# Forget-gate terms of two heads in pairs on separate row groups, and forget logits from split weights

## The chip, the cores and the metric

The kernel runs on one core of a Trainium2 chip. The metric is the device time of one execution in microseconds (us), the median over runs. The engines are PE (TensorE matmuls; PEld its weight loads), DVE (VectorE), ACT (ScalarE), POOL (GpSimd) and SP (SyncE, which issues most of the DMAs).

## What is computed

Two transformer blocks in sequence, two layers each, on 256 tokens (the second block adds 256 context tokens) of width 1024, all float32. The change touches the second layer of the first block alone. Its mixer has eight MoBA heads and eight "forgetting" heads of 64 columns:

```
qc, kc, vc, qd, kd, vd, fd = split(h @ w_in)
log_f = log_sigmoid(fd + forget_b)            # one logit per token and head: (256, 8)
cum   = cumsum(log_f, over the tokens)
s     = qd @ kd.T * scale + cum[:, q_pos, None] - cum[:, None, :]
od    = softmax(where(k_pos <= q_pos, s, -inf)) @ vd
```

## The kernel before, in words

**Products in two halves.** Large products are not done in float32. Activations and weights are each split into a high half (`HH`, `WH`, type fp32r) and a low half (`HL`, `WL`, the rest), and `product` (line 847) issues three matmuls: high by high, high by low, low by high. Weights come as chunks of 1024 x 256 floats into a ring of four raw buffers (`RAWS`); SP loads chunk n into slot n % 4 once chunk n - 4 is used up (`wait_slot`, line 656). A chunk has four pieces of two row tiles. For each piece ACT makes the high half (line 1168), DVE the low half (line 640), and PE multiplies; there are four piece buffers, so ACT and DVE work one chunk ahead of PE.

**Hosted work.** Between the chunks of a stage SP also loads chunks of the adaptive-norm matrices ("ada", 1 MB each). DVE folds them in itself (lines 1456 and 1459), a quarter after each piece it splits, and only then frees the slot.

**The projection of the second layer** (`qkv`, lines 576 to 579) goes through the items q0, q2, forget, k0, k2, v0, v256, q4, q6, k4, k6 and two more v. Ada chunks follow q0, q2, k0, k2, v0, v256 and q4 in the ring. The forget item is a chunk of 8 columns. PE (lines 924 to 931) multiplies it unsplit, in float32: for each of 8 row tiles one matmul with the high and one with the low half of the activations, 16 in all, then gives the slot back (`forget_used`). It waits for nothing but the chunk's landing. ACT then takes the logits out of PSUM and does the exponential and logarithm (`forget_logs`, lines 1317 to 1323); DVE does the rest and the running sum (`forget_cum`, lines 1653 to 1665), and gives `fg_cum`. Both do so in the order of the items, that is between the splits of k0 and those of k2.

**The attention** (`attn`; PE line 1053, ACT line 1337, DVE line 1694) runs over halves: a half is two heads (hh = 0, 1) and one block of 128 queries (qt = 0 with 128 keys, qt = 1 with 256). The two heads of a half lie on rows 0 to 63 and 64 to 127 of `QB` and `KB`, and their scores go to two PSUM banks. PE's order is written out: scores of half i + 2, transposes of half i, values of half i - 1. For the last eight halves (`FORGET`) the bias is added by matmuls over 8 rows: `sel` (one row of -1, line 1067) by the negated sums `NCUM` adds the query-independent part over all keys, and `CUM` by `sel` adds the other part, 128 keys at a time. `CUM`, `NCUM` and `NEGSEL` lie on rows 0 to 7 for both heads. The terms of a head follow its scores, then comes the other head (lines 1061 to 1071). DVE takes a head's row minimum with the causal mask as soon as that head's `scores` count is given (line 1723).

**POOL** runs through its stages by itself: the low halves after a norm (line 806), one DMA of `NEGSEL` in the second layer's projection (line 830), and nothing in the attention of that layer.

In the float32 matmuls of this trace one matmul has two records (x2 is one matmul), in fp32r products one.

Of the kernel before, what the change touches and what calls it, by code (L numbers as in the profile page):

```python
# [25 lines left out]
F32 = mybir.dt.float32  # L26
F32R = mybir.dt.float32r
ALU = mybir.AluOpType
# [229 lines left out]
def _build(nc, ctx, a, c, out):  # L258
    def sem(name):
        return ctx.enter_context(nc.semaphore(name))  # L260


    def sb(name, shape, dt=F32):
        return ctx.enter_context(nc.sbuf_tensor(name, shape, dt))
# [25 lines left out]
    SINK = sb("sink", [P, 16])  # L290
    LAM = sb("lam", [P, 8])
    FB = sb("forget_bias", [8, 1])
    NSINK = sb("neg_sink", [P, 16])
    MX = sb("min_part", [P, 4])
    NM = sb("neg_max", [P, 4])
# [51 lines left out]
    FD_ABS = PR[0:8, 0, T:2 * T]  # L347
    FD_MIN = PR[0:8, 1, 0:T]
    FD_ONE = PT[0:8, 0, 0:2, :]
    CUM = BT[0:8, 8 * T:9 * T]  # L350
    NCUM = BT[0:8, 9 * T:10 * T]
    NEGSEL = BT[0:8, 10 * T:10 * T + 8 * P].rearrange("h (a p) -> h a p", a=8)

    BANK = [ctx.enter_context(nc.psum_tensor(f"bank{b}", [P, 512], F32)) for b in range(8)]
    PAIR = [(BANK[0], BANK[1]), (BANK[2], BANK[3])]
# [29 lines left out]
    bias_in = Tally(sem("bias_in"))  # L385
    fg_x, fg_abs, fg_exp = sem("forget_logit"), sem("forget_abs"), sem("forget_exp")
    fg_cum, fg_sel = sem("forget_cum"), sem("forget_select")
    qn_sq, qn_sums, qn_root = Tally(sem("qknorm_sq")), Tally(sem("qknorm_sums")), Tally(sem("qknorm_root"))
    qn_mm, qn_out, qn_rstd = Tally(sem("qknorm_spread")), Tally(sem("qknorm_out")), sem("qknorm_rstd")
    rope_mm, rope_out = Tally(sem("rope_mm")), Tally(sem("rope_out"))  # L390
# [375 lines left out]
    @block.gpsimd  # L766
    def _(pool):
        chain = Chain(pool, pool_chain)

        def const(dst, src):  # L770
            pool.dma_start(dst, src).then_inc(const_in, 16)

        def setup():
            for t in credited:
                pool.sem_inc(t.sem, t.credit)
            const(head_cols[:, :], c["head_cols"])
            const(rotate[:, :], c["rotate"])
            const(ONEHOT[:, :], c["bucket_onehot"])
            const(T5MASK[:, :], c["t5_neg_mask"])
            const(TABLE[:, 0:12], a["rel_bias"])  # L780
            const(TABLE[:, 12:20], a["rel_bias"][:, 0:8])
            const(SINK[:, :], a["wa_sink_2"].rearrange("l h -> (l h)").rearrange("(o n) -> o n", o=1)
                  .broadcast_to([P, 16]))
            const(FB[:, :], a["forget_b"].rearrange("l h -> h l"))
            const(LROW[:, :, :], a["diff_lambda"].broadcast_to([P, 4, HD]))

            chain.link(pool.memset(RPB[:, :, :, :], 0.0))
            for l in range(2):
                pool.dma_start(RPB[:, l, :, 48:48 + RPB_W],
                               a["na_rpb_2"][l, :, 4:4 + NA_ROWS, :]).then_inc(skew_src, 16)  # L790
            pool.wait_ge(skew_src, 32)
            for l in range(2):
                src = RPB[:, l, :, :].rearrange("h i w -> h (i w)")
                pool.dma_start(na_lines[l * NA_H:(l + 1) * NA_H, :], src).then_inc(skew_out, 16)

            pool.wait_ge(t5_rows, 1)
            pool.dma_start(t5_dram.rearrange("r n l -> n r l"),
                           T5ROW[:, None, :].broadcast_to([N_T5, T5_COPIES, BIAS_L])).then_inc(skew_out, 16)
        def low(s):

            def tile(at):
                par = at.u % 2
                t = at(lambda k: k)
                pool.wait_ge(mod_hi.sem, at(lambda k: s.hi + k + 1))
                pool.wait_ge(mod_t2.sem, at(lambda k: s.t2 + k + 1))  # L805
                pool.tensor_tensor(HL[:, bass.ds(t, 1), 0:s.n], T2[:, par:par + 1, 0:s.n],  # L806
                                   HH[:, bass.ds(t, 1), 0:s.n].bitcast(F32), ALU.subtract
                                   ).then_inc(h_ready.sem, 1)
            each(pool, 0, 8, 2, tile)

        def ffn_in(s):

            def step(at):
                t = at(lambda k: 2 * k)
                pool.wait_ge(act_hi.sem, at(lambda k: s.hi + k + 1))
                pool.tensor_tensor(AL[:, bass.ds(t, 2), 0:s.n], T2[:, :, 0:s.n],  # L816
                                   AH[:, bass.ds(t, 2), 0:s.n].bitcast(F32), ALU.subtract
                                   ).then_inc(act_ready.sem, 1)
            each(pool, 0, 10, unroll(s), step)
            step(At(None, 10, 1, 1))  # L820

        for s in PLAN:
            if s.kind == "setup":
                setup()
            elif s.kind in ("mod", "ln", "rms") and not s.last_ln:
                low(s)
            elif s.kind == "ffn_in":
                ffn_in(s)
            elif s.kind == "qkv" and s.layer == 1:
                pool.dma_start(NEGSEL, c["neg_select"].rearrange("h (a p) -> h a p", a=8)).then_inc(fg_sel, 16)  # L830
            elif s.kind == "attn":
                if s.sub:

                    pool.wait_ge(skew_out, 48)
                    pool.dma_start(na_dram, na_lines.rearrange("h w -> (h w)").rearrange("(o n) -> o n", o=1)
                                   .broadcast_to([64, NA_LINE])).then_inc(na_out, 16)
# [4 lines left out]
    def _(pe):  # L841
# [78 lines left out]
        def qkv(s):  # L920
            for it in s.items:
                ch, grp = it.chunk, it.grp
                ready = modulated(s.ready) if it is s.items[0] else None
                if it.what[0] == "forget":
                    wait_landed(pe, one, lambda _: ch)
                    w = raw_ap(ch.n, KC, 8)
                    for k in range(KC):
                        mm(B_STAT[0:8, 0:T], w[:, k, :], HH[:, k, 0:T].bitcast(F32), k == 0, False)
                        ins = mm(B_STAT[0:8, 0:T], w[:, k, :], HL[:, k, 0:T].bitcast(F32), False, k == KC - 1)
                    ins.then_inc(forget_used, 1)  # L930
                    continue
                wait_bank(one, lambda _: grp)
                pair = PAIR[grp.n % 2]
# [119 lines left out]
        def attn(s):  # L1053
            def score(h):
                nk, at = P * h.nb, h.qoff + P * h.qt
                forget = h in FORGET
                if h is FORGET[0]:
                    pe.wait_ge(fg_cum, 2)
                    pe.wait_ge(fg_sel, 16)
                pe.wait_ge(exp_done.sem, h.ex - 2)  # L1060
                for hh in range(2):
                    half = slice(HD * hh, HD * hh + HD)
                    o = BANK[2 * (h.n % 2) + hh]
                    ins = mm(o[:, 0:nk], QB[half, h.q, at:at + P], KB[half, h.k, h.koff:h.koff + nk], True,
                             not forget)
                    if forget:
                        sel = NEGSEL[:, 2 * h.p + hh, :]
                        mm(o[:, 0:nk], sel, NCUM[:, 0:nk], False, False)
                        for b in range(h.nb):
                            ins = mm(o[:, P * b:P * b + P], CUM[:, P * h.qt:P * h.qt + P], sel, False, b == h.nb - 1)  # L1070
                    ins.then_inc(scores.sem, 1)

            def turn(h):
                for k in range(h.slots):
# [82 lines left out]
    def _(act):  # L1157
# [96 lines left out]
        def qkv(s):  # L1254
            if s.layer == 0:

                act.wait_ge(skew_out, 48)
            for it in s.items:
                if it.what[0] == "forget":
                    forget_logs()  # L1260
                    continue
                for p in it.chunk.pieces:
                    ahead(one, lambda _: p, split, late)
                used(one, lambda _: it.chunk.pieces[-1])
                pair, kind, n = PAIR[it.grp.n % 2], it.what[0], it.n
                if kind in "qk":
# [49 lines left out]

        def forget_logs():

            act.wait_ge(forget_used, 1)
            act.activation(FD, B_STAT[0:8, 0:T], ACT.Identity, bias=FB[:, 0:1]).then_inc(fg_x, 1)  # L1320
            act.wait_ge(fg_abs, 1)
            chain.link(act.activation(FD_ABS, FD_ABS, ACT.Exp, scale=-1.0))
            act.activation(FD_ABS, FD_ABS, ACT.Ln, bias=1.0).then_inc(fg_exp, 1)
# [97 lines left out]
    def _(dve):  # L1421
# [231 lines left out]
        def forget_cum():  # L1653
# [5 lines left out]
            dve.wait_ge(fg_exp, 1)  # L1659
            chain.link(dve.drain())  # L1660
            chain.link(dve.tensor_tensor(FD_MIN, FD_MIN, FD_ABS, ALU.subtract))
            dve.tensor_tensor_scan(CUM, FD_ONE.rearrange("p a b -> p (a b)"), FD_MIN, 0.0, ALU.mult, ALU.add
                                   ).then_inc(fg_cum, 1)
            dve.wait_ge(fg_cum, 1)
            dve.tensor_scalar(NCUM, CUM, -1.0, None, ALU.mult).then_inc(fg_cum, 1)

        def qk_norm(s):

# [106 lines left out]
        for s in PLAN:  # L1775
# [11 lines left out]
                    dve.wait_ge(ada_out, s.need)  # L1787
                norm(s)
            elif s.kind == "qkv":
                for it in s.items:  # L1790
                    if it.what[0] == "forget":
                        forget_cum()
                        continue
                    ahead_of(one, lambda _: it.chunk, (lambda _: it.host) if it.host else None)
                if s.hosted:
                    close(s.hosted)
            elif s.kind == "ffn_in":
# [37 lines left out]
```

## Time and profile before

| | |
|---|---|
| median of 3 runs | 2935.88 us (2933.57 to 2938.0) |
| the profiled execution | 2934.27 us |
| its span | 2932.5 us |
| PE busy | 2669.5 us, 91% |
| PE weight loads | 2241.6 us, 76% |
| DVE busy | 1757.8 us, 60% |
| ACT busy | 1081.4 us, 37% |
| POOL busy | 224.9 us, 8% |
| mean granted TensorE clock | 0.926 of full speed |
| DMA | 413.91 MB, mean 141 GB/s |

The profile is of one execution. Busy time is what an engine's instructions took; matmuls overlap in it. The granted clock is the share of TensorE's full speed (2.4 GHz) that the throttle allowed: 1.00 or, at its other level (1.2 GHz), 0.50. A bracket at the end of a timeline line gives the idle time of the engine before it and what ended that. Times in timelines count from the start of the span. A row of stretches has: the stretch, its length, the busy time (and instructions) of PE, PEld, DVE, ACT and POOL, the granted clock, the mean busy share of the 16 DMA engines and the GB/s moved.

### The profile page before, as it was taken

The numbers are of one execution on the slowest core, as the hardware profiler recorded it, in microseconds if no ns is written. First come the engines' busy times: TensorE is split into PE (matmuls) and PEld (weight loads), VectorE is DVE, ScalarE is ACT, GpSimd is POOL, SyncE is SP. The second block draws the span as 40 slices with busy tenths as digits, with TensorE's granted clock in tenths as the row PEclk, the third lists the DMA queues.
The fourth block names the chain that finished last, engine by engine and source line by source line (L and its number), as shares of the span: only waits on it lengthen the run. The fifth ranks groups of instructions, "written<-read, shape, count | busy, mean of one in ns | idle before, by whom it ended". The sixth has DMA issues, their size and how long they took to land. (4 is left out here: it accounts for less than half of the span.)

```text
span 2932.5 us, 39627 instructions
## 1 busy us (share of the span) xinstructions
PE 2669.5 (91%) x15387; PEld 2241.6 (76%) x15387; DVE 1757.8 (60%) x3177; ACT 1081.4 (37%) x2061; POOL 224.9 (8%) x167
## 2 busy tenths in 40 slices
PE   4768998998998799998999889999899998988899
PEld 4747997867998588886855668888688886856899
DVE  6567776537776655545748566544655433647654
ACT  2343543433443323223326442322333322316553
POOL 2000100000100201101000020000111000100110
PEclk8867998967999899999989999999999999879999
DMA  8924774903676144332720134443244433720453
GB/s 287 279 84 144 254 255 130 270 29 102 232 243 200 51 150 144 126 122 83 214 72 1 44 100 130 137 133 119 93 145 135 138 120 116 214 72 24 142 178 133
DMA packets 355603, 413.91 MB, mean 141 GB/s; under 512 B 25707, under 2 KB 292628, under 8 KB 355352
## 3 DMA queue, kind: packets, MB, share of 16 engines
q1 hardware_dynamic: 353326, 404.37, 43.3%
q0 software_dynamic: 736, 4.58, 0.5%
q8 instruction: 122, 2.00, 0.3%
q10 hardware_dynamic: 1354, 2.43, 0.2%
q14 instruction: 65, 0.53, 0.1%
HBM read 409.75 MB, written 5.27 MB: 142 GB/s over the span
## 5 line engine op out<-in xcount | busy, mean ns | idle before, releaser
L640 DVE TENSOR_TENSOR weight_lo<-raw_weights,weight_hi 128x512 fp32r<-128x512 f32 x1024 | 778.1, 767 | 929.6 <-ACT weight_hi L1168 919.6
L1168 ACT ACTIVATE weight_hi<-raw_weights 128x512 fp32r<-128x512 f32 x1024 | 633.0, 629 | 1326.2 <-PE bank L845 1192.5
L845 PE MATMUL bank<-H_hi,weight_hi 128*128 128x256 f32 (+1 forms) x2832 | 975.0, 344 | 109.6 <-POOL H_lo L806 77.6
L845 PE MATMUL bank<-H_lo,weight_hi 128*128 128x256 f32 (+1 forms) x2832 | 956.4, 338 | 0.0
L845 PE MATMUL bank<-H_hi,weight_lo 128*128 128x256 f32 (+1 forms) x2832 | 956.4, 338 | 0.0
L845 PEld LDWEIGHTS bank<-H_hi,weight_hi 128*128 128x128 f32 x2832 | 558.0, 197 | 187.6 <-issue 112.6
L845 PEld LDWEIGHTS bank<-H_hi,weight_lo 128*128 128x128 f32 x2832 | 558.4, 197 | 50.7
L845 PEld LDWEIGHTS bank<-H_lo,weight_hi 128*128 128x128 f32 x2832 | 559.7, 198 | 48.7 <-issue 0.5
L1459 DVE SCALAR_TENSOR_TENSOR ada_partial<-raw_weights,silu_c,ada_partial 128x512 f32<-128x512 f32 x616 | 441.5, 743 | 1.3 <-DVE ada_partial L1459 0.2
L845 PE MATMUL bank<-hidden_hi,weight_hi 128*128 128x256 f32 (+1 forms) x1056 | 359.0, 340 | 3.8 <-DVE weight_lo L640 3.8
L845 PE MATMUL bank<-hidden_hi,weight_lo 128*128 128x256 f32 (+1 forms) x1056 | 354.1, 335 | 0.0
L845 PE MATMUL bank<-hidden_lo,weight_hi 128*128 128x256 f32 (+1 forms) x1056 | 352.0, 333 | 0.0
L845 PEld LDWEIGHTS bank<-hidden_hi,weight_hi 128*128 128x128 f32 x1056 | 198.4, 188 | 25.3 <-DVE weight_lo L640 4.1
L845 PEld LDWEIGHTS bank<-hidden_hi,weight_lo 128*128 128x128 f32 x1056 | 198.3, 188 | 23.2
L845 PEld LDWEIGHTS bank<-hidden_lo,weight_hi 128*128 128x128 f32 x1056 | 198.0, 188 | 23.5 <-issue 1.4
L806 POOL TENSOR_TENSOR H_lo<-tmp,H_hi 128x256 fp32r<-128x256 f32 (+1 forms) x80 | 92.3, 1154 | 1587.4 <-ACT tmp L1250 1549.6
L816 POOL TENSOR_TENSOR hidden_lo<-tmp,hidden_hi 128x1024 fp32r<-128x1024 f32 (+1 forms) x66 | 121.9, 1848 | 1028.1 <-ACT hidden_hi L1290 1028.1
L845 PEld LDWEIGHTS bank<-ones,ada_partial 128*128 128x128 f32 x704 | 91.9, 204 | 20.8 <-DVEq L1464 18.8
L845 PE MATMUL bank<-ones,ada_partial 128*128 128x1 f32 x704 | 88.6, 252 | 18.3 <-DVEq L1464 18.3
L845 PE MATMUL bank<-tmp,ones 128*128 128x512 f32 (+1 forms) x164 | 74.9, 603 | 30.0 <-ACT tmp L1216 29.8
L1081 PEld LDWEIGHTS bank<-ident,probs 128*128 128x128 f32 x404 | 48.8, 155 | 69.4 <-issue 65.4
L1290 ACT ACTIVATE hidden_hi<-tmp 128x1024 fp32r<-128x1024 f32 (+1 forms) x66 | 55.9, 847 | 121.7 <-DVE tmp L1599 121.7
(165 smaller groups left out, 2124.4 us busy)
## 6 DMA issues: line engine op xcount, KB each, us to landing
raw_weights<-in_w_ada_dram SPq DMA_DIRECT2D x120, 1024.0 KB, 5.4
raw_weights<-in_w_ffn_up_dram SPq DMA_DIRECT2D x88, 1024.0 KB, 5.2
raw_weights<-in_w_ffn_in_dram SPq DMA_DIRECT2D x44, 1024.0 KB, 5.4
raw_weights<-in_w_ffn_down_dram SPq DMA_DIRECT2D x32, 1024.0 KB, 5.3
raw_weights<-in_w_in_dram SPq DMA_DIRECT2D x18, 1024.0 KB, 8.3
raw_weights<-in_w_ffn_out_dram SPq DMA_DIRECT2D x16, 1024.0 KB, 7.7
raw_weights<-in_w_in_ab_dram SPq DMA_DIRECT2D x12, 1024.0 KB, 9.4
raw_weights<-in_w_in_cd_dram SPq DMA_DIRECT2D x12, 1024.0 KB, 7.7
```

Source lines behind the costliest of these rows:

```text
L640: eng.tensor_tensor(WL[:, p.g % SPLIT, 0:p.kt * CW].rearrange("p (t n) -> p t n", n=CW), raw_ap(ch.n, ch.kt, CW)[:, p.k0:p.k0 + p.kt, :], ...
L806: pool.tensor_tensor(HL[:, bass.ds(t, 1), 0:s.n], T2[:, par:par + 1, 0:s.n], HH[:, bass.ds(t, 1), 0:s.n].bitcast(F32), ALU.subtract).then_ ...
L816: pool.tensor_tensor(AL[:, bass.ds(t, 2), 0:s.n], T2[:, :, 0:s.n], AH[:, bass.ds(t, 2), 0:s.n].bitcast(F32), ALU.subtract).then_inc(act_re ...
L845: return pe.matmul(o, w, x, start=start, stop=stop, skip_group_check=True)
L1081: ins = pe.transpose(bank[:, col:col + P], PR[:, 2 * (h.n % 2) + hh, P * b:P * b + P], ident[:, :])
L1168: act.activation(WH[:, p.g % SPLIT, 0:p.kt * CW].rearrange("p (t n) -> p t n", n=CW), raw_ap(ch.n, ch.kt, CW)[:, p.k0:p.k0 + p.kt, :], ACT ...
L1290: act.activation(AH[:, bass.ds(t, 2), 0:n], T2[:, :, 0:n], ACT.Copy).then_inc(act_hi.sem, 1)
L1459: ins = dve.scalar_tensor_tensor(out=acc, in0=w[:, k, :], scalar=SILU_C[:, i:i + 1], in1=acc, op0=ALU.mult, op1=ALU.add)
```

## The change

Four things:

- **Second copies.** `CUM`, `NCUM` and `NEGSEL` become lists of two: the first on rows 0 to 7 as before, the second on rows 64 to 71. POOL loads `NEGSEL` twice, then waits for the running sums (`fg_cum`) and copies them with a DMA to the second place. PE waits for all three DMAs (`fg_sel` 48).
- **Order of the terms.** PE issues both heads' scores first, then the terms alternating between the heads, head 1 from the second copy. Both heads' `scores` counts are given with the last pair.
- **Forget logits.** ACT makes a high half `FH` of the 8-column chunk after the splits of k0, DVE the low half `FL` after its splits of k0 and the hosted ada work, and gives `forget_used`. PE waits for that and issues the three fp32r matmuls of `product` per row tile, 24 in all.
- **Signals.** `forget_used` now comes from DVE; a new `fg_mm` from PE releases ACT's `forget_logs`.

```diff
-    CUM = BT[0:8, 8 * T:9 * T]
-    NCUM = BT[0:8, 9 * T:10 * T]
-    NEGSEL = BT[0:8, 10 * T:10 * T + 8 * P].rearrange("h (a p) -> h a p", a=8)
+    CUM = [BT[r:r + 8, 8 * T:9 * T] for r in (0, HD)]
+    NCUM = [BT[r:r + 8, 9 * T:10 * T] for r in (0, HD)]
+    CUMS = [BT[r:r + 8, 8 * T:10 * T] for r in (0, HD)]
+    NEGSEL = [BT[r:r + 8, 10 * T:10 * T + 8 * P].rearrange("h (a p) -> h a p", a=8) for r in (0, HD)]
...
             elif s.kind == "qkv" and s.layer == 1:
-                pool.dma_start(NEGSEL, c["neg_select"].rearrange("h (a p) -> h a p", a=8)).then_inc(fg_sel, 16)
+                for sel in NEGSEL:
+                    pool.dma_start(sel, c["neg_select"].rearrange("h (a p) -> h a p", a=8)).then_inc(fg_sel, 16)
+                pool.wait_ge(fg_cum, 2)
+                pool.dma_start(CUMS[1], CUMS[0]).then_inc(fg_sel, 16)
...
                 if it.what[0] == "forget":
-                    wait_landed(pe, one, lambda _: ch)
-                    w = raw_ap(ch.n, KC, 8)
+                    pe.wait_ge(forget_used, 1)
                     for k in range(KC):
-                        mm(B_STAT[0:8, 0:T], w[:, k, :], HH[:, k, 0:T].bitcast(F32), k == 0, False)
-                        ins = mm(B_STAT[0:8, 0:T], w[:, k, :], HL[:, k, 0:T].bitcast(F32), False, k == KC - 1)
-                    ins.then_inc(forget_used, 1)
+                        ins = product(B_STAT[0:8, 0:T], k, FH[:, k, :], FL[:, k, :], HH[:, k, 0:T], HL[:, k, 0:T],
+                                      k == 0, k == KC - 1)
+                    ins.then_inc(fg_mm, 1)
                     continue
...
-                    pe.wait_ge(fg_sel, 16)
+                    pe.wait_ge(fg_sel, 48)
                 pe.wait_ge(exp_done.sem, h.ex - 2)
+                o = [BANK[2 * (h.n % 2) + hh] for hh in range(2)]
                 for hh in range(2):
                     half = slice(HD * hh, HD * hh + HD)
-                    o = BANK[2 * (h.n % 2) + hh]
-                    ins = mm(o[:, 0:nk], QB[half, h.q, at:at + P], KB[half, h.k, h.koff:h.koff + nk], True,
+                    ins = mm(o[hh][:, 0:nk], QB[half, h.q, at:at + P], KB[half, h.k, h.koff:h.koff + nk], True,
                              not forget)
-                    if forget:
-                        sel = NEGSEL[:, 2 * h.p + hh, :]
-                        mm(o[:, 0:nk], sel, NCUM[:, 0:nk], False, False)
-                        for b in range(h.nb):
-                            ins = mm(o[:, P * b:P * b + P], CUM[:, P * h.qt:P * h.qt + P], sel, False, b == h.nb - 1)
-                    ins.then_inc(scores.sem, 1)
+                    if not forget:
+                        ins.then_inc(scores.sem, 1)
+                if forget:
+                    sel = [NEGSEL[hh][:, 2 * h.p + hh, :] for hh in range(2)]
+                    for hh in range(2):
+                        mm(o[hh][:, 0:nk], sel[hh], NCUM[hh][:, 0:nk], False, False)
+                    for b in range(h.nb):
+                        for hh in range(2):
+                            ins = mm(o[hh][:, P * b:P * b + P], CUM[hh][:, P * h.qt:P * h.qt + P], sel[hh], False,
+                                     b == h.nb - 1)
+                            if b == h.nb - 1:
+                                ins.then_inc(scores.sem, 1)
...
+                if i + 1 < len(s.items) and s.items[i + 1].what[0] == "forget":
+                    forget = s.items[i + 1].chunk
+                    wait_landed(act, one, lambda _: forget)
+                    act.activation(FH[:, :, :], raw_ap(forget.n, KC, 8), ACT.Copy).then_inc(fg_hi, 1)
                 used(one, lambda _: it.chunk.pieces[-1])
...
         def forget_logs():
 
-            act.wait_ge(forget_used, 1)
+            act.wait_ge(fg_mm, 1)
...
                     ahead_of(one, lambda _: it.chunk, (lambda _: it.host) if it.host else None)
+                    if i + 1 < len(s.items) and s.items[i + 1].what[0] == "forget":
+                        dve.wait_ge(fg_hi, 1)
+                        dve.tensor_tensor(FL[:, :, :], raw_ap(s.items[i + 1].chunk.n, KC, 8),
+                                          FH[:, :, :].bitcast(F32), ALU.subtract).then_inc(forget_used, 1)
```

The rest declares `FH`, `FL` and the two semaphores, and writes the sums to the first copies.

## Rows read from the trace of the kernel before

**Rows 1.** Stretches: the attention's heads without forget terms, then with.

```profile
593.70:609.40 15.70, 13.13 (x79) 7.70 (x79) 10.06 (x53) 9.55 (x35) 0.00 (x0) 0.67 0.20 67
609.40:658.70 49.30, 49.30 (x178) 33.35 (x176) 13.78 (x62) 10.08 (x40) 0.00 (x0) 0.53 0.00 1
```

**Rows 2.** Timeline of PE, forget heads: start, us, line, names, tile, records.

```profile
609.38 0.49 PE L845 MATMUL bank<-k,q 64*128 64x128 f32 x2
...
611.48 0.44 PE L1081 MATMUL bank<-ident,probs 128*128 128x128 f32 x2
...
620.29 0.79 PE L845 MATMUL bank<-k,q 64*128 64x128 f32 x2
621.02 1.22 PE L845 MATMUL bank<-bias 8*128 8x128 f32 x4
...
624.03 0.69 PE L1081 MATMUL bank<-ident,probs 128*128 128x128 f32 x2
...
625.70 1.22 PE L845 MATMUL bank<-k,q 64*128 64x256 f32 x2
626.85 2.07 PE L845 MATMUL bank<-bias 8*128 8x256 f32 x6
...
632.00 1.11 PE L1081 MATMUL bank<-ident,probs 128*128 128x128 f32 x4
```

**Rows 3.** Timeline of PE, scores of two heads without forget terms.

```profile
601.03 0.80 PE L845 MATMUL bank<-k,q 64*128 64x128 f32 x4
601.76 0.69 PE L1081 MATMUL bank<-ident,probs 128*128 128x128 f32 x2
...
603.43 1.23 PE L845 MATMUL bank<-k,q 64*128 64x256 f32 x4
604.59 1.11 PE L1081 MATMUL bank<-ident,probs 128*128 128x128 f32 x4
```

**Rows 4.** Timeline of PE, end of q2, forget logits, start of k0.

```profile
516.66 0.28 PE L845 MATMUL bank<-H_lo,weight_hi 128*128 128x256 f32 x1
516.78 0.28 PE L845 MATMUL bank<-H_hi,weight_lo 128*128 128x256 f32 x1
516.99 0.60 PE L845 MATMUL bank<-H_hi,raw_weights 128*8 128x256 f32 x2
...
523.99 0.39 PE L845 MATMUL bank<-H_hi,weight_hi 128*128 128x256 f32 x1
```

**Rows 5.** Timeline of DVE around the forget logits.

```profile
518.27 0.15 DVE L1491 TENSOR_TENSOR ada<-bank,b_ada_cols 128x4 f32<-128x4 f32 x1
...
522.13 0.74 DVE L1459 SCALAR_TENSOR_TENSOR ada_partial<-raw_weights,silu_c,ada_partial 128x512 f32<-128x512 f32 x1
...
529.61 0.69 DVE L640 TENSOR_TENSOR weight_lo<-raw_weights,weight_hi 128x512 fp32r<-128x512 f32 x1
...
533.75 0.75 DVE L1459 SCALAR_TENSOR_TENSOR ada_partial<-raw_weights,silu_c,ada_partial 128x512 f32<-128x512 f32 x1
```

**Rows 6.** Timeline of ACT: the logits taken out, the splits of k2.

```profile
524.10 0.47 ACT L1320 ACTIVATE probs<-bank,forget_bias 8x256 f32<-8x256 f32 x1 [4.38 <-PE bank L845]
...
528.95 2.19 ACT L1168 ACTIVATE weight_hi<-raw_weights 128x512 fp32r<-128x512 f32 x4 [0.93 <-DMA raw_weights<-in_w_in_cd_dram]
```

**Rows 7.** Stretches of the first layer's projection: a gap of PE, then after it.

```profile
106.64:110.11 3.47, 0.00 (x0) 0.03 (x1) 0.83 (x3) 1.50 (x3) 0.00 (x0) 1.00 1.05 254
110.80:114.20 3.40, 3.40 (x19) 3.40 (x18) 3.40 (x6) 0.48 (x2) 0.00 (x0) 0.50 1.09 323
114.20:117.60 3.40, 3.40 (x31) 3.40 (x30) 0.45 (x2) 0.82 (x2) 0.00 (x0) 0.99 0.69 157
```

**Rows 8.** Timeline of SP: the ada chunk that waits for the one after k0.

```profile
534.58 0.39 SPq L694 DMA_DIRECT2D raw_weights<-in_w_ada_dram  x1
```

**Rows 9.** Stretches of the second layer's projection after the logits.

```profile
524.00:542.00 18.00, 15.61 (x130) 15.43 (x130) 10.94 (x21) 9.33 (x17) 0.00 (x0) 1.00 1.07 301
542.00:545.00 3.00, 3.00 (x28) 3.00 (x27) 1.43 (x3) 0.20 (x1) 0.00 (x0) 1.00 0.66 142
```

More of the change, by code:

```diff
@@ L292, in _build @@
     FB = sb("forget_bias", [8, 1])
+    FH = sb("forget_hi", [P, KC, 8], F32R)
+    FL = sb("forget_lo", [P, KC, 8], F32R)
     NSINK = sb("neg_sink", [P, 16])
@@ L387, in _build @@
     fg_cum, fg_sel = sem("forget_cum"), sem("forget_select")
+    fg_hi, fg_mm = sem("forget_hi_done"), sem("forget_logits")
     qn_sq, qn_sums, qn_root = Tally(sem("qknorm_sq")), Tally(sem("qknorm_sums")), Tally(sem("qknorm_root"))
@@ L1257, in qkv @@
                 act.wait_ge(skew_out, 48)
-            for it in s.items:
+            for i, it in enumerate(s.items):
                 if it.what[0] == "forget":
@@ L1661, in forget_cum @@
             chain.link(dve.tensor_tensor(FD_MIN, FD_MIN, FD_ABS, ALU.subtract))
-            dve.tensor_tensor_scan(CUM, FD_ONE.rearrange("p a b -> p (a b)"), FD_MIN, 0.0, ALU.mult, ALU.add
+            dve.tensor_tensor_scan(CUM[0], FD_ONE.rearrange("p a b -> p (a b)"), FD_MIN, 0.0, ALU.mult, ALU.add
                                    ).then_inc(fg_cum, 1)
             dve.wait_ge(fg_cum, 1)
-            dve.tensor_scalar(NCUM, CUM, -1.0, None, ALU.mult).then_inc(fg_cum, 1)
+            dve.tensor_scalar(NCUM[0], CUM[0], -1.0, None, ALU.mult).then_inc(fg_cum, 1)
         def qk_norm(s):
@@ L1789, in _ @@
             elif s.kind == "qkv":
-                for it in s.items:
+                for i, it in enumerate(s.items):
                     if it.what[0] == "forget":
```

## The prediction, made before the changed kernel was run

> **What bounds the kernel now.** The busy table gives PE 91% of the span, but that is a mean over stages, so I went to the two stages that the change touches: first the table of stretches, then PE's timeline in each, then DVE, ACT and SP around the logits.
>
> In the attention with forget terms PE is busy in all of its 49.3 us, while DVE is busy for 13.78 and ACT for 10.08 [rows 1]. The clock granted there is 0.53, so nearly all of it runs at the lower level. PE's own sequence is the bound, and what is cut from it comes off the end. The DMA engines stand still there (share 0.00): the raw ring is full, the next stage has its weights, and no transfer can take back what is won.
>
> In the projection, the forget logits hold PE for 7.00 us, from 516.99 to 523.99, at the full clock [rows 4]. What comes after is paced otherwise: from 524 to 542 the DMA engines are busy without a break (share 1.07, 301 GB/s), and PE has 2.4 us of idle time [rows 9].
>
> **The terms, step by step.** One half with 128 keys takes from 620.29 to 624.03, so 3.74 us for two heads; of a head's 1.87 the scores are 0.73 (620.29 to 621.02) and the terms 1.14. One with 256 keys takes 6.30 (625.70 to 632.00), the scores of a head 1.15 and its terms 2.00 [rows 2]. There are eight halves: the first, at the full clock, takes 2.10 (609.38 to 611.48), three more like 3.74, four like 6.30. Sum: 2.10 + 11.22 + 25.20 = 38.5 us.
>
> What does a pair cost that lies on rows 0 and 64? The trace has no pair of terms, but it has pairs of scores: heads without forget terms issue theirs side by side, and two heads take 0.73 with 128 keys (601.03 to 601.76) and 1.16 with 256 (603.43 to 604.59) [rows 3]. That is what one head takes alone in rows 2. Each of these matmuls loads its own 128 weight columns, as the terms do, so it is the nearest row. Bounds: from complete overlap, as here, to none. I take complete overlap: 0.73 + 1.14 = 1.87 for a half with 128 keys, 1.16 + 2.00 = 3.16 with 256, 1.05 for the first. Sum: 1.05 + 3 x 1.87 + 4 x 3.16 = 19.3. **Saved: 19.2 us**, all on PE's path.
>
> Is something else late then? Four pairs of halves in 49.3 - 19.2 = 30.1 us leave DVE at 46% and ACT at 33%. Before the forget heads the same attention passes eight halves in 15.7 us with 10.06 us of DVE work [rows 1], so these engines keep up with twice the pace. Head 0's minimum now starts with head 1's, at the end of the half, but its probabilities are wanted only after the scores of two more halves. I cost that at nothing; without that cover it would be a row minimum, under 0.5 us a half.
>
> **The copies.** POOL's two more DMAs and its wait for the sums stall its queue until about 533. Behind them is the next norm's low half, after the attention. The sums are done by 529.61 [rows 5], the first term is due at 609.38 [rows 2]: 80 us hide a copy of 16 KB. Cost: nothing.
>
> **The logits.** Before, PE went from q2 straight to the logits, since these wait for no split. While it did so, ACT and DVE split k0. Now PE waits for `FL`, which stands behind all four splits of k0 and the hosted ada work on DVE; the last of that starts at 522.13 and lasts 0.74, to 522.87 [rows 5]. `FH` on ACT is covered, since ACT idles for 4.38 us before the logits come out [rows 6]. `FL` has 64 columns: between the 0.15 us of a 4-column operation and the 0.69 of a 512-column split [rows 5]; near the small one, 0.2. So PE starts at about 523.1, after a gap of 6.1 us which replaces work.
>
> The 24 products stream 256 columns like q2's, which come every 0.12 us at the full clock (516.66 to 516.78) [rows 4]: 2.9 us. The other bound is the 0.44 of the unsplit ones (7.00 / 16), 10.5 us. I take q2's pace, for the type and the width are the same. But the clock will have fallen: after a gap of 3.47 us in the first layer's projection the granted clock went to 0.50 for the next 3.40 us, with 19 products in them where the following 3.40 us have 31 [rows 7]. So 24 products take 24 x 3.40 / 19 = 4.3 us or somewhat more (twice 0.12 each would be 5.8); I take 5.0, to 528.1.
>
> A rule of the Trainium skill bears on this (TensorE: Matmul & The Clock Gate, "Why this matters for your kernels"): idle gaps of PE between bursts of matmuls are to be avoided, as the clock drops to half. It speaks against this edit, and without it the sum would have the products end at 526.0 rather than 528.1.
>
> Then ACT takes the logits out at 528.2 instead of 524.10 [rows 6], and DVE's running sum ends some 4.1 us later. In DVE's queue the splits of k2 stand behind it (529.61) and, with them, the ada chunk whose end releases SP's next ada load (534.58) and, after that, v256's [rows 5, 8]. Those loads start 4.1 us later on a queue that had no slack, but the DMA engines lose less then further on, where before they were busy for only 0.66 of 3.0 us against 1.07 (1.2 us lost) [rows 9]. 4.1 - 1.2 = 2.9. PE's slower k0 (48 products at the low clock, some 3.4 us more by rows 7) hides under the loads; with that cover gone it adds up to 3.4. Bounds: 0.8 (full clock: 2.0 - 1.2) to 6.3; a gain is excluded, since PE now starts the logits when six sevenths of them were done before. I take **2.5 us lost**, a little under 2.9 since PE's idle time later in that stretch can soak up some.
>
> **Sum.** -19.2 + 2.5 = -16.7 us. Against the profiled execution: 2934.27 - 16.7 = 2917.6. That execution lies 1.6 under the median of 2935.88, so the forecast is **2919.2 us**.
>
> **Rivals.**
>
> *The weight loads of a pair do not overlap.* By rows 2 a 128-column term costs 0.57 and a 256-column one 0.86, so 0.28 of each is not streaming. If that part stayed serial, two pairs in a half of 128 keys and three in one of 256 would give back (3 x 2 + 4 x 3 + 1) x 0.28 = 5.3 us: 2924.5. Against it: the scores' pairs load as much and show none of it [rows 3]. For it: the terms use 8 rows, not 64. The same page of the Trainium skill, in "Measured speedup vs the span model", has four row tiles at 3.07 times one; an estimate for two at that share of the ideal, 1.53, makes the saving 13.4 us. No row here shows such a loss. Chance 12%.
>
> *The clock rises in the shorter stage.* Denser work may hold the full level longer: the heads without terms had 0.67 [rows 1]. 30.1 x 0.53 / 0.67 = 23.8, so 6.3 us more saved: 2912.9. Against it: the terms still make up a third of what is left. 12%.
>
> *The pairs run one after the other.* Nothing is saved, the logits cost 2.5: 2938.4, no measurable change. Then the change does not do what it says. 8%.
>
> *Slower: each turn from one row group to the other costs.* A head's first 128-column matmul after a change of kind takes 0.73 where a term takes 0.57: 0.16. If the alternating terms paid that at every turn and did not overlap, a half of 128 keys would have 4 turns instead of 2, one of 256 6 instead of 2: 3 x 0.32 + 0.16 + 4 x 0.64 = 3.7, with the logits 6.2: 2942.1. It decides from 0.15 a turn. Against it: the scores turn without cost [rows 3]. 4%.
>
> **How the numbers follow.** The forecast has 64%; its own range is 2915 to 2923 (the logits' bounds below, and some 2 us of clock steps that fall at other moments above). The two rivals on its sides take the range to **2911 and 2927**; left out are the serial pairs and the turns, 12%, and tails. 0.2% (5.9 us) is about what a measurement of this kernel can tell from no change: faster 0.88 (64 + 12 + 12), same 0.08, slower 0.04.
>
> **What would show it.** In the changed profile a forget half with 128 keys should take PE about 1.9 us and one with 256 about 3.2 at the low clock, the stage about 30 us. Before the 128*8 products PE should idle for about 6 us with DVE's `FL` as releaser, then run at 0.50; the logits should come out about 4 us later against q2's end, and the time from there to the first scores should grow by 1 to 4 us. I am wrong if the terms' records follow each other with the gaps of now (serial), if DVE or ACT ends PE's waits in the stage, or if the delay of the logits reaches the attention in full.

## The result, and the profile of the changed kernel

The kernel took 2912.95 us (median of 4 runs, 2907.77 to 2916.71) against 2936.94 for the one before on the same chip: a ratio of 0.9918, 95% interval 0.9899 to 0.9936. Measured again later, it took 2916.66 against 2934.79, ratio 0.9936 (0.9923 to 0.9948). So 18 to 24 us were won where 16.7 were forecast, and both medians lie in the range. The profiled execution took 2916.71 us, with a span of 2914.9, PE busy for 2634.1 us and a mean clock of 0.934. DVE (1756.6 us) and ACT (1082.2) did the same work as before.

**The attention.** The first two stretches answer to [rows 1]; the other two cut the second at the step of the clock.

```profile
602.70:618.40 15.70, 13.43 (x78) 7.78 (x78) 10.04 (x53) 9.49 (x35) 0.00 (x0) 0.67 0.22 67
618.40:642.70 24.30, 23.83 (x181) 16.22 (x177) 12.40 (x62) 10.17 (x40) 0.00 (x0) 0.73 0.01 2
618.40:629.60 11.20, 10.73 (x109) 7.57 (x105) 7.87 (x40) 6.49 (x25) 0.00 (x0) 1.00 0.01 2
629.60:642.70 13.10, 13.10 (x73) 8.65 (x73) 4.53 (x24) 3.68 (x15) 0.00 (x0) 0.50 0.01 1
```

The forget heads take 24.3 us instead of 49.3. PE is still busy nearly throughout, so it still bounds the stage. But 11.2 of the 24.3 us ran at the full clock. The second stretch of [rows 1], cut in the same way, had 3.2 of 49.3:

```profile
609.40:612.60 3.20, 3.20 (x25) 2.38 (x24) 2.50 (x12) 1.87 (x9) 0.00 (x0) 1.00 0.02 5
612.60:658.70 46.10, 46.10 (x154) 30.97 (x154) 11.28 (x51) 8.21 (x33) 0.00 (x0) 0.50 0.00 1
```

PE's timeline in that stage, which answers to [rows 2]:

```profile
618.45 0.49 PE L852 MATMUL bank<-k,q 64*128 64x128 f32 x4
618.87 0.71 PE L852 MATMUL bank<-bias 8*128 8x128 f32 x8
619.74 0.43 PE L1093 MATMUL bank<-ident,probs 128*128 128x128 f32 x2 [0.16 <-DVE probs L1758]
...
631.15 1.23 PE L852 MATMUL bank<-k,q 64*128 64x256 f32 x4
632.30 2.08 PE L852 MATMUL bank<-bias 8*128 8x256 f32 x12
634.31 1.11 PE L1093 MATMUL bank<-ident,probs 128*128 128x128 f32 x4
...
635.98 0.80 PE L852 MATMUL bank<-k,q 64*128 64x128 f32 x4
636.71 1.22 PE L852 MATMUL bank<-bias 8*128 8x128 f32 x8
637.86 0.69 PE L1093 MATMUL bank<-ident,probs 128*128 128x128 f32 x2
...
644.95 0.66 PE L1093 MATMUL bank<-ident,probs 128*128 128x128 f32 x2 [0.51 <-DVE probs L1758]
```

A group now holds both heads (x12 where it was x6) and takes what one head took: 2.08 us against 2.07 for the terms over 256 keys, 1.22 against 1.22 for 128. At the low clock a half lasts 1.88 us (635.98 to 637.86) or 3.16 (631.15 to 634.31). PE now waits for DVE four times, which it did not before: 0.16 us in three of the halves at the full clock, and 0.51 us just behind the stage, at the transposes of the last half but one (the last row).

**The logits.** PE, between q2 and k0 (the first record is the last of q2):

```profile
517.63 0.28 PE L852 MATMUL bank<-H_hi,weight_lo 128*128 128x256 f32 x1
527.53 0.38 PE L852 MATMUL bank<-H_hi,forget_hi 128*8 128x256 f32 x1 [9.62 <-DVE forget_lo L1813]
...
531.71 0.28 PE L852 MATMUL bank<-H_hi,weight_hi 128*128 128x256 f32 x1
```

DVE in that time, which answers to [rows 5]:

```profile
526.36 0.75 DVE L1475 SCALAR_TENSOR_TENSOR ada_partial<-raw_weights,silu_c,ada_partial 128x512 f32<-128x512 f32 x1
527.25 0.23 DVE L1813 TENSOR_TENSOR forget_lo<-raw_weights,forget_hi 128x64 fp32r<-128x64 f32 x1
532.41 0.41 DVE L1671 SCALAR_TENSOR_TENSOR probs<-probs 8x256 f32<-8x256 f32 x1 [4.93 <-ACT probs L1336]
...
537.35 0.67 DVE L644 TENSOR_TENSOR weight_lo<-raw_weights,weight_hi 128x512 fp32r<-128x512 f32 x1
```

ACT ([rows 6]):

```profile
521.23 2.19 ACT L1180 ACTIVATE weight_hi<-raw_weights 128x512 fp32r<-128x512 f32 x4 [8.69 <-DMA raw_weights<-in_w_in_cd_dram]
...
531.91 0.47 ACT L1336 ACTIVATE probs<-bank,forget_bias 8x256 f32<-8x256 f32 x1 [7.81 <-PE bank L852]
```

PE waits for `FL`, as forecast, and `FL` stands behind the last piece of ada work. From k0's first split on ACT (521.23) to the first product are 6.3 us, the forecast 6.1. The gap is 9.62 us and not 6.1 because PE was through with q2 3.3 us before k0 landed; in the kernel before the two fell together. In q2 the granted clock rose to 1.00 at 506.8 here and at 513.6 there. That part of the program is the same in both, and the wait costs nothing by itself, since `FL` counts from k0's landing.

**Where the time went.** DVE makes the same 1024 low halves of weights in the same order in both kernels. The table has the start of the nth one, less its start in the profile of the kernel before: how far a kernel is behind (+) or ahead (-) at that point, in us. The kernels of the experiments below stand beside the change.

```
                      q2     k2     v256   q6     k4     before   after    last
                                                  3rd    attn     attn
before, at (us)       505.7  529.6  545.5  562.2  568.4  592.8    669.9    2919.3
change                +4.2   +7.7   +6.5   +6.5   +8.8   +8.9    -15.7    -17.6
e6_same_kernel        +1.0   +4.5   +3.3   +2.8   +5.3   +5.4    -15.9    -14.6
e2_logits_only        +0.8   +4.4   +3.0   +2.4   +5.0   +5.1     +6.9     +6.9
e3_same_rows          -2.8   +0.9   -0.0   -0.6   +1.9   +2.0    -12.5    -11.2
e5_no_turns           +1.9   +5.3   +3.9   +3.3   +4.5   +4.6    -14.9    -15.9
e1_pairs_only         -0.1   -0.2   -0.5   -0.8   -0.8   -0.8    -22.2    -22.1
e8_pairs_again        -2.6   -1.9   -2.1   -2.8   -1.5   -1.4    -24.2    -25.2
e4_fl_early           -0.4   +0.0   +0.0   -0.8   -0.8   -0.8    -27.6    -27.7
e7_early_again        +1.1   +1.3   +1.4   +0.6   +2.0   +2.1    -19.2    -20.3
```

In the first column no changed work has been done yet: -2.8 to +4.2 is what one execution differs from another by. From there the change loses 4.7 us up to the attention, wins 24.6 in it and 1.9 after it.

### The profile page after: what moved, and what is told of

The parts are those of the page before. It is cut to its first block and busy times, and to the rows that moved or that the text cites. A ratio compares the mean times of both kernels' runs of the same rounds, so it can differ in the third digit from the quotient of the medians.

```text
span 2914.9 us, 39615 instructions
## 1 busy us (share of the span) xinstructions
PE 2634.1 (90%) x15379; PEld 2218.6 (76%) x15379; DVE 1756.6 (60%) x3178; ACT 1082.2 (37%) x2062; POOL 226.3 (8%) x169
```

## The experiments

Each kernel is the changed one with an edit; the diffs are against it. Each was timed beside the kernel before on the same chip, e1 to e4 in one series (before: 2933.90 us) and e5 to e8 in another (before: 2934.79 us).

### Pairs alone, unsplit logits

```diff
-                    pe.wait_ge(forget_used, 1)
+                    wait_landed(pe, one, lambda _: ch)
+                    w = raw_ap(ch.n, KC, 8)
...
-                        ins = product(B_STAT[0:8, 0:T], k, FH[:, k, :], FL[:, k, :], HH[:, k, 0:T], HL[:, k, 0:T],
-                                      k == 0, k == KC - 1)
+                        mm(B_STAT[0:8, 0:T], w[:, k, :], HH[:, k, 0:T].bitcast(F32), k == 0, False)
+                        ins = mm(B_STAT[0:8, 0:T], w[:, k, :], HL[:, k, 0:T].bitcast(F32), False, k == KC - 1)
...
-                    act.activation(FH[:, :, :], raw_ap(forget.n, KC, 8), ACT.Copy).then_inc(fg_hi, 1)
...
-                        dve.tensor_tensor(FL[:, :, :], raw_ap(s.items[i + 1].chunk.n, KC, 8),
-                                          FH[:, :, :].bitcast(F32), ALU.subtract).then_inc(forget_used, 1)
```

> The terms in pairs, the logits as before the change. Theory: the pairs alone save 25 us and the split logits lose 4 to 5, so this kernel is 23 to 28 us faster than before, about 2909, and faster than the whole change by about 4; the logits come out of PSUM 7 us after q2's end, the DVE split of k2 follows as before. Rival (the split logits help, or cost nothing): no faster than the whole change, 2913 or above.

Measured: 2909.23 us, ratio 0.9921 (0.9906 to 0.9935). That is 24.7 us faster, as expected. The table has no loss in the projection (-0.1 to -0.8) and 21.4 us won in the attention.

### Split logits alone, terms as before

```diff
-                for sel in NEGSEL:
-                    pool.dma_start(sel, c["neg_select"].rearrange("h (a p) -> h a p", a=8)).then_inc(fg_sel, 16)
-                pool.wait_ge(fg_cum, 2)
-                pool.dma_start(CUMS[1], CUMS[0]).then_inc(fg_sel, 16)
+                pool.dma_start(NEGSEL[0], c["neg_select"].rearrange("h (a p) -> h a p", a=8)).then_inc(fg_sel, 16)
...
+                    if forget:
+                        sel = NEGSEL[0][:, 2 * h.p + hh, :]
+                        mm(o[:, 0:nk], sel, NCUM[0][:, 0:nk], False, False)
+                        for b in range(h.nb):
+                            ins = mm(o[:, P * b:P * b + P], CUM[0][:, P * h.qt:P * h.qt + P], sel, False, b == h.nb - 1)
+                    ins.then_inc(scores.sem, 1)
```

> The logits from split weights, the terms as before the change. Theory: PE idles for 6 to 10 us behind the forget weights' low half, the two ada and q/k/v loads after the running sums are issued 3 to 4 us later, and the kernel is 3 to 6 us slower than before, 2940 to 2943. Rival 1 (the loads set the pace and hide it): within 1 us of before. Rival 2 (fewer PE cycles count): 2 to 4 us faster.

Measured: 2937.65 us, ratio 1.0020 (1.0012 to 1.0029): this half of the change is slower by itself, by 3.75 us, within the 3 to 6 us expected. PE shows the same gap as in the whole change:

```profile
514.22 0.28 PE L849 MATMUL bank<-H_hi,weight_lo 128*128 128x256 f32 x1
524.12 0.38 PE L849 MATMUL bank<-H_hi,forget_hi 128*8 128x256 f32 x1 [9.62 <-DVE forget_lo L1804]
```

It loses 4.3 us up to the attention. Its forget stage lasts 49.4 us, as before: the split logits do nothing to it.

### Both heads' terms on the first rows

```diff
-                    sel = [NEGSEL[hh][:, 2 * h.p + hh, :] for hh in range(2)]
+                    sel = [NEGSEL[0][:, 2 * h.p + hh, :] for hh in range(2)]
...
-                        mm(o[hh][:, 0:nk], sel[hh], NCUM[hh][:, 0:nk], False, False)
+                        mm(o[hh][:, 0:nk], sel[hh], NCUM[0][:, 0:nk], False, False)
...
-                            ins = mm(o[hh][:, P * b:P * b + P], CUM[hh][:, P * h.qt:P * h.qt + P], sel[hh], False,
+                            ins = mm(o[hh][:, P * b:P * b + P], CUM[0][:, P * h.qt:P * h.qt + P], sel[hh], False,
```

> The whole change, but both heads' terms read the first copies, so that they alternate on the same rows 0 to 7. Theory (the row groups make the gain): a forget half at the low clock takes PE 3.6 to 3.8 us with 128 keys and 6.1 to 6.4 with 256, the stage stays near 49 us and 0.53 clock, and the kernel is 3 to 6 us slower than before, about 2941. Rival (the order makes it, with one change from scores to terms in a half instead of two): half or more of the 25 us is kept, 2925 or below.

Measured: 2925.44 us, ratio 0.9974 (0.9964 to 0.9984). PE's timeline, two halves at the low clock:

```profile
626.03 0.80 PE L852 MATMUL bank<-k,q 64*128 64x128 f32 x4
626.76 2.07 PE L852 MATMUL bank<-bias 8*128 8x128 f32 x8
628.76 0.69 PE L1093 MATMUL bank<-ident,probs 128*128 128x128 f32 x2
...
630.43 1.23 PE L852 MATMUL bank<-k,q 64*128 64x256 f32 x4
631.59 3.78 PE L852 MATMUL bank<-bias 8*128 8x256 f32 x12
635.29 1.11 PE L1093 MATMUL bank<-ident,probs 128*128 128x128 f32 x4
```

The expectation missed. The terms do run one after the other: 3.70 us (631.59 to 635.29) for two heads where the change takes 2.01. But a half lasts 4.86 us and not 6.1 to 6.4, since the scores of the two heads, which lie on rows 0 and 64 anyway, now stand next to each other and overlap: 1.16 us for two, where they took 2.30 apart. The expectation had left them at one head after the other, though [rows 3] shows that neighbours overlap. The terms gain too, from 4.00 to 3.70 us: they now follow the scores once in a half instead of twice. So the new *order* brings 1.44 of the 3.14 us that a half with 256 keys wins (6.30 - 4.86; 1.14 from the scores, 0.30 from the terms), and the second row group the other 1.70. With 128 keys the order brings 1.01 of 1.86 (3.74 to 2.73). The whole stage takes 36.7 us, 12.6 less than before, so the order alone keeps half of the 25.0 that the change won there, about as the rival had it (2925 or below; the median is 0.44 above).

### The forget chunk split ahead of k0's

```diff
-                for p in it.chunk.pieces:
-                    ahead(one, lambda _: p, split, late)
                 if i + 1 < len(s.items) and s.items[i + 1].what[0] == "forget":
...
+                for p in it.chunk.pieces:
+                    ahead(one, lambda _: p, split, late)
...
-                    ahead_of(one, lambda _: it.chunk, (lambda _: it.host) if it.host else None)
                     if i + 1 < len(s.items) and s.items[i + 1].what[0] == "forget":
...
+                    ahead_of(one, lambda _: it.chunk, (lambda _: it.host) if it.host else None)
```

> The whole change, with the forget weights' two halves made one item earlier, ahead of k0's splits, so that PE need not wait for them. Theory: PE goes from q2 to the 24 products without a gap, the logits come out about 3 us after q2's end instead of 7, the lost 4 to 5 us come back and little more is won, since the loads set the pace after: 2907 to 2910, level with the pairs alone within 2 us. Rival (the loss was in the products or elsewhere, not in the wait): 2912 or above.

Measured: 2907.48 us, ratio 0.9913 (0.9898 to 0.9928). DVE makes `FL` before k0 lands:

```profile
510.48 0.23 DVE L1812 TENSOR_TENSOR forget_lo<-raw_weights,forget_hi 128x64 fp32r<-128x64 f32 x1
517.66 0.69 DVE L644 TENSOR_TENSOR weight_lo<-raw_weights,weight_hi 128x512 fp32r<-128x512 f32 x1 [6.95 <-ACT weight_hi L1180]
```

and PE goes on without a gap, at the full clock:

```profile
516.36 0.28 PE L852 MATMUL bank<-H_hi,weight_lo 128*128 128x256 f32 x1
516.47 0.28 PE L852 MATMUL bank<-H_hi,forget_hi 128*8 128x256 f32 x1
...
519.20 0.28 PE L852 MATMUL bank<-H_hi,weight_hi 128*128 128x256 f32 x1
```

As expected, what was lost comes back. The 24 products take 2.7 us instead of 7.0, and the loss at k2 is gone (+0.0). Nothing is won either: k2's split on ACT starts at 528.99, against 528.95 [rows 6], and it waits for its DMA:

```profile
528.99 2.19 ACT L1180 ACTIVATE weight_hi<-raw_weights 128x512 fp32r<-128x512 f32 x4 [3.37 <-DMA raw_weights<-in_w_in_cd_dram]
```

The unsplit logits were hidden: behind them ACT still idled 0.93 us for the same DMA [rows 6].

### The second head's terms after the first's

```diff
                     for hh in range(2):
                         mm(o[hh][:, 0:nk], sel[hh], NCUM[hh][:, 0:nk], False, False)
-                    for b in range(h.nb):
-                        for hh in range(2):
+                        for b in range(h.nb):
                             ins = mm(o[hh][:, P * b:P * b + P], CUM[hh][:, P * h.qt:P * h.qt + P], sel[hh], False,
```

> The whole change, but after the second head's first term all 128-column terms of head 0 come before those of head 1; rows and copies as in the change. Theory (two row groups work side by side, but PE takes its matmuls in order, so only neighbours on different rows overlap): in a half of 128 keys there is one term of 128 columns for each head, so its order stays as it was and it stays at 1.88 us; in one of 256 keys the order 0,1,0,0,1,1 leaves one term of 0.57 us more without a partner on each side: 3.16 + about 0.6 = 3.7 us for four halves, so 2 to 3 us more than the change, 2915 to 2916. Rival (PE looks ahead past a waiting matmul, or the order is of no matter): 3.16 us, the change's own time, 2913. Rival (each turn from one row group to the other costs something): fewer turns, so shorter than 3.16 us.

Measured: 2918.62 us against 2916.66 for the change in the same series, ratios 0.9939 (0.9917 to 0.9960) and 0.9936: the times do not tell them apart. PE's timeline does:

```profile
622.18 1.23 PE L852 MATMUL bank<-k,q 64*128 64x256 f32 x4
623.33 3.09 PE L852 MATMUL bank<-bias 8*128 8x256 f32 x12
626.35 1.11 PE L1092 MATMUL bank<-ident,probs 128*128 128x128 f32 x4
...
628.02 0.80 PE L852 MATMUL bank<-k,q 64*128 64x128 f32 x4
628.75 1.23 PE L852 MATMUL bank<-bias 8*128 8x128 f32 x8
629.91 0.69 PE L1092 MATMUL bank<-ident,probs 128*128 128x128 f32 x2
```

A half with 128 keys stays at 1.89 us; one with 256 takes 4.17 instead of 3.16, its terms 3.02 (623.33 to 626.35) instead of 2.01. The stage takes 31.2 us, against the 27.3 of the next experiment, with the full clock for nearly as long (6.5 and 6.6 us): the four halves of 256 keys make the difference.

The expectation does not describe its own edit. The 128-column terms now stand in the first loop over the heads, so *all* terms of head 0 come before those of head 1: 0,0,0,1,1,1 with 256 keys, not 0,1,0,0,1,1, and 0,0,1,1 with 128 keys, where it said that nothing changes. If only neighbours in that order overlapped, head 1's terms with 128 keys would start with head 0's second, and the four would take about 1.14 + 0.57 = 1.71 us. They take 1.16 (628.75 to 629.91), what one head takes alone. With 256 keys PE has these records of the terms between 623.45 and 624.60 (by shape; x is their number, then busy us and mean ns):

```profile
L852 PE MATMUL bank<-bias 8*128 8x256 f32 x3 | 1.8, 736 | 0.0
L852 PE MATMUL bank<-bias 8*128 8x128 f32 x2 | 0.6, 416 | 0.0
```

A term has two records, so the third of 256 columns is head 1's. It has begun here, with only two of the four 128-column records of head 0, which all come before it in the kernel's order. So the theory that only neighbours overlap falls, and the rival that PE looks ahead past a waiting matmul holds, though not without limit: in both kinds of half head 1's first term passed one term of head 0 and not two (with 256 keys it started 1.02 us after head 0's first, the time of one 256-column term). How far PE looks in other orders was not tried. The rival with a price for each turn falls too: with 128 keys there is one turn from head to head in the kernel's order instead of three, at the same time within 0.01 us.

### The changed kernel again

> The changed kernel itself, unaltered, for a second profile. If what the attention saves beyond the row groups comes from the moments at which the clock happens to step, the halves again take 1.88 and 3.16 us at the low level, the stage again has about 17.7 us of work counted at full clock, but its share at full clock differs from the 11.2 of 24.3 us of the first profile (the kernels with pairs so far had 6.5 to 13.8 us) and its length with it, between 21 and 29 us. If the full clock follows from the order of the work alone, 11 us and 24.3 us again. The logits again cost 4 to 5 us, 2911 to 2915 in all.

Measured: 2916.66 us, ratio 0.9936 (0.9923 to 0.9948). The stage, in two stretches:

```profile
616.40:623.00 6.60, 6.44 (x68) 4.53 (x66) 4.79 (x25) 4.00 (x16) 0.00 (x0) 1.00 0.02 4
623.00:643.70 20.70, 20.70 (x116) 13.67 (x114) 7.42 (x36) 6.20 (x25) 0.00 (x0) 0.50 0.00 1
```

The same program takes 27.3 us here and 24.3 in the first profile, with 6.6 and 11.2 us at the full clock. The work, counted at the full clock (the low part halved), is 17.0 and 17.7 us. So the full clock does not follow from the order of the work alone. The median lies 1.7 us above the 2911 to 2915 expected.

### The early split and the pairs alone, again

The same edits as in e4 and e1.

> The change with the split of the forget chunk ahead of k0's splits, a second time, beside the change itself and the pairs alone. Theory (the wait for that split behind k0's is all that the logits cost, 4.6 us): 4 to 5 us under the change, 2907 to 2909, and the offset of DVE's splits at the end of the projection within 1 us of the kernel before. Rival (the first difference was chance of the clock in the attention): the same time as the change within 2 us.

> The pairs alone with the unsplit logits, a second time, beside the change and the early split. Theory: 4 to 5 us under the change and within 2 us of the early split, 2907 to 2910; the split logits bring no time of their own, since the 4 us by which their products are shorter are spent where PE waits for k0's landing anyway. Rival (the shorter products pay): 2 to 4 us slower than the early split.

Measured: 2908.48 us, ratio 0.9912 (0.9898 to 0.9925), for the early split; 2909.91, 0.9915 (0.9902 to 0.9929), for the pairs alone. Both lie 7 to 8 us under the change of the same series, more than the 4 to 5 expected. For the early split the table gives the logits 3.4 us of the 8.2: 1.0 us lost from q2 to the attention against 4.4. Another 2.4 us lie behind the attention, where the programs are the same; chance between executions is likely there, but the rest has no place in these profiles. The early split and the pairs alone are within 2 us of each other in both series: the split logits bring no time of their own here. Of the versions tried, the early split had the lowest medians, by less than the intervals tell apart, and the edit to keep is the pairs.

## Why the prediction was right, and where its terms were off

**The terms in pairs: the mechanism held exactly, the clock was mis-sized.** The step "I take complete overlap" gave 1.87 and 3.16 us for a half at the low clock; measured are 1.88 and 3.16. At the clock of before the stage would be what was forecast: e6's work, counted at the full clock, is 6.6 + 20.7 / 2 = 16.95 us, and with only 3.2 of it done at that level the stage lasts 3.2 + 2 x 13.75 = 30.7 us (forecast 30.1), a saving of 18.6 (forecast 19.2). What came on top is more time at the full clock, as in the rival with the clock. The full level lasted 3.2 us into this stage in the kernel before and in e2. With full pairs it lasted 6.5 or 6.6 us in four profiles (e1, e6, e7, e8), 11.2 in the first of the change and 13.8 in e4. Against the 30.7 us the stage is 3.1 to 3.5 us shorter in the four, and 6.4 and 8.5 (24.3 and 22.2 us) in the other two.

In the ten profiles two things go with the moment at which the clock falls. One is the order of the work: in e2 and e6 the clock rose 0.2 us before the stage (at 616.0 and 616.2), and it fell 3.2 and 6.6 us into it; e3 and e5 have 6.6 and 6.5 us too, so full pairs are not needed. The other is the execution: e4 and e7 are the same program, with 13.8 and 6.5 us. What ties the clock to either was not tried. The argument "the terms still make up a third of what is left" was no reason against the rival. As a case of its own it had 12%; some 3 us of it should have been part of the likeliest one.

**Weight loads, turns, serial pairs: fallen.** No part of a pair was serial, and e5 excludes a price for turns. The 0.28 us "not streaming" in each term, worked out from [rows 2], is not there. In e3, four terms of 128 columns take 2.00 us (626.76 to 628.76), and two of 256 with four of 128 take 3.70 (631.59 to 635.29): that is 0.43 us for each 128 columns and 0.30 once for all. By the prediction's prices these were 2.28 and 4.00. The Trainium skill's figure of 3.07 for four row tiles (TensorE: Matmul & The Clock Gate, "Measured speedup vs the span model") is of another packing, which no run here has. The estimate of 1.53 for two that was worked out from it is not what this case shows: two heads' terms take 2.08 us where one head's took 2.07, a factor of 2.0.

**What else is late: one us at most.** The later minimum was costed at nothing, since the scores of two more halves cover it. At the full clock that cover was a little short (three waits of 0.16 us), and the last two halves have none: one wait of 0.51 us, in all six profiles with full pairs. So DVE does end PE's waits, which the prediction named as a sign of being wrong, but they are small. The copies cost nothing. POOL waits for the sums without anything behind it:

```profile
510.19 1.10 POOL L835 DMA_DIRECT2D bias<-const_neg_select_dram  x2
537.71 0.81 POOL L837 DMA_DIRECT2D bias<-bias  x1 [26.42 <-DVE bias L1681]
```

The copy is issued 81 us before the first term (618.87).

**The logits: the chain held link by link, and one link was missing.** The products started 6.3 us after k0's first split (forecast 6.1). They took 4.2 us (taken as 5.0), since the clock rose again at 530.6, before the last nine, and the logits came out 10.7 us after that split (531.91 less 521.23). Before, those were 7.1 us: 524.10 [rows 6] less the start of this row of ACT's timeline:

```profile
517.00 2.19 ACT L1168 ACTIVATE weight_hi<-raw_weights 128x512 fp32r<-128x512 f32 x4 [8.01 <-DMA raw_weights<-in_w_in_cd_dram]
```

So they were 3.6 us late, not 4.1. In the table k2 less q2 is 3.5 us, v256 less q2 2.3 (both for the change and for e6). So 1.2 us were regained on the way to v256, the size forecast for the dip of the DMA engines; whether the dip gave them was not tried. The step that failed is the last: "a little under 2.9 since PE's idle time later in that stretch can soak up some". Instead, about 2.5 us were lost again between q6 and k4. These stretches of e6 show where:

```profile
517.20:524.30 7.10, 0.00 (x0) 0.00 (x0) 5.44 (x10) 2.88 (x7) 0.00 (x0) 0.50 0.46 139
524.30:527.40 3.10, 3.05 (x15) 1.88 (x16) 0.00 (x0) 0.00 (x0) 0.00 (x0) 0.50 0.72 206
557.00:565.00 8.00, 6.36 (x55) 6.27 (x53) 4.00 (x8) 1.45 (x4) 0.00 (x0) 1.00 1.08 294
565.00:571.80 6.80, 6.00 (x28) 6.03 (x29) 5.54 (x9) 3.11 (x7) 0.00 (x0) 0.50 0.83 240
```

and the same work in the kernel before, 2.8 us earlier:

```profile
554.20:562.20 8.00, 6.37 (x55) 6.28 (x53) 4.01 (x8) 1.47 (x4) 0.00 (x0) 1.00 1.04 290
562.20:569.00 6.80, 5.99 (x50) 6.02 (x51) 6.65 (x11) 3.94 (x8) 0.00 (x0) 1.00 0.74 218
```

The first two rows are the gap and the products after it, at 0.50, as the prediction had it. By the Trainium skill's rule on idle gaps (TensorE: Matmul & The Clock Gate, "Why this matters for your kernels") the clock was to be low there; the trace agrees. The last row of e6 was not foreseen. PE has waited 2.45 us for q6's first split, as its timeline has it:

```profile
565.80 0.55 PE L852 MATMUL bank<-H_hi,weight_hi 128*128 128x256 f32 x1 [2.45 <-DVE weight_lo L644]
```

and in the stretch the clock is at 0.50, with 28 matmuls. In the kernel before the same wait, 2.44 us, stands in a stretch at the full clock, with 50:

```profile
563.01 0.36 PE L845 MATMUL bank<-H_hi,weight_hi 128*128 128x256 f32 x1 [2.44 <-DVE weight_lo L640]
```

In e6 the clock falls at 565.0, before that wait is over. The size of the loss between q6 and k4 goes with the length of the stretch at 0.50 there, in all ten profiles: 6.8 us of it and 2.3 to 2.6 us lost in the change, e2, e3 and e6; 3.4 us and 1.2 to 1.4 lost in e5, e7 and e8; none and 0.0 in the kernel before, e1 and e4. All five profiles that have the delay are among those that lose; of the five without it two are, with the shorter stretch. So the clock accounts for this loss; that the delay brings the low clock is likely by these numbers, but was not tried. Together the links make the 4.3 to 4.8 us of the table (e5: 2.8); the term was 2.5, and its upper bound of 6.3 held it. By the prediction's own sign, "if the delay of the logits reaches the attention in full", this term was wrong: 3.6 us late at the logits, 4.4 to 4.7 at the attention.

**The sum.** The attention won more than forecast (21.3 to 24.6 us in the two profiles of the change, not 19.2) and the logits cost more (4.4 to 4.7, not 2.5). The errors offset each other in part, so the prediction came out better than its terms, and that is luck. The first median, 2912.95, lies below the 2915 to 2923 of the likeliest case, where the rival with the clock had put it (2912.9); the second, 2916.66, lies inside.

## What to carry to other kernels

Here matmuls over 8 and over 64 rows overlapped completely when neighbours in PE's order lay on different row groups. Look for the order first (it alone gave nearly half of what a half wins, 1.44 of 3.14 us), then for the second copy. Price a stage that PE bounds at both clock levels and state what share of it each has: a shorter stage may keep the full level for longer. When a product begins to depend on a split, put that split where its input lands, not where the order of the items has it: behind the next chunk's splits it cost some 4 us that one place earlier did not.

## What the runs showed of the hardware that was not expected

The same program, with the same work in the same order, ran its forget stage in 24.3 and in 27.3 us, by the moment at which the clock fell (11.2 or 6.6 us into it); another program did so in 22.2 and 27.2 us (e4 and e7, 13.8 and 6.5). One profile of such a stage does not give its length to better than some 5 us. A wait of PE of 2.44 us stood in a stretch at the full clock in one profile, and one of 2.45 us in another where the clock fell to 0.50 for 6.8 us. And PE did not start the float32 terms in the kernel's order: one on free rows passed one on busy rows, by one term (e5).
